# A two-block transformer prologue in fp32: modulation summed beside the projections, differential attention beside the value and half the output projection

## The reference

```python
z, xbc, dt_raw, q, k, v = split_cols(h @ w_in, EVEN_SPLITS)      # h = norm(x) * (1 + scale) + shift
y_ssd = ssd_mixer(z, xbc, dt_raw, conv_w, conv_b, dt_bias, A_log, D_skip, ssd_norm)
y_diff = diff_attention(q, k, v, lam, diff_norm, rel_bias, layer_idx)
return jnp.concatenate([y_ssd, y_diff], axis=-1) @ w_out

# diff_attention, causal, 8 heads, two maps m of 64 features each
logits = einsum("bqhmd,bkhmd->bhmqk", q_blk, k32) + bias[None, :, None]
p = softmax(where(dist >= 0, logits, -inf))
attn = p[:, :, 0] - lam_full * p[:, :, 1]
out = rms_norm(einsum("bhqk,bkhe->bqhe", attn, v32), subln_w) * (1.0 - lam_init)
```

## Time and profile before

| what | us |
|---|---|
| device time, median of 3 runs | 4331.51 (4325.75 to 4333.39) |
| the profiled execution | 4334.11 |
| its span, first to last instruction | 4332.2 |
| TensorE busy in the span | 3752.1 (87%) |
| VectorE, ScalarE, GpSimd busy | 1823.6, 1319.7, 457.8 |
| granted TensorE clock, mean | 0.887 |
| moved by DMA | 313.45 MB |

### The profile page before, as it was taken

One profiled execution on the slowest core, in us unless ns is written; L12 is line 12 of the kernel. 1 busy time (PEld: TensorE's weight loads), 2 busy tenths in 40 slices (PEclk: granted clock), 3 DMA queues, 4 the chain that ended last, 5 costly groups with the idle time before them and its releaser, 6 DMA issues. The chain is left out here.

```text
span 4332.2 us, 48721 instructions
## 1 busy us (share of the span) xinstructions
PE 3752.1 (87%) x19465; PEld 2867.3 (66%) x19465; DVE 1823.6 (42%) x2952; ACT 1319.7 (30%) x2062; POOL 457.8 (11%) x401
## 2 busy tenths in 40 slices
PE   4599866999999479999599887999979988889998
PEld 4487644788868346888466643778856764467886
DVE  5635435333332343332345243445345424344434
ACT  0133224323232233232332233334233114333333
POOL 0000100011000310110113000031001310003100
PEclk6599986999999859999799696999989978689998
DMA  7622110222221002221210001232212100023221
GB/s 281 240 74 69 34 50 32 104 78 88 87 92 54 20 29 88 98 91 65 87 54 31 21 1 54 67 108 88 98 49 73 31 22 1 31 76 102 88 97 39
DMA packets 226412, 313.45 MB, mean 72 GB/s; under 512 B 11925, under 2 KB 151070, under 8 KB 225438
## 3 DMA queue, kind: packets, MB, share of 16 engines
q1 hardware_dynamic: 226206, 310.54, 21.3%
HBM read 306.83 MB, written 3.68 MB: 72 GB/s over the span
## 5 line engine op out<-in xcount | busy, mean ns | idle before, releaser
L373 PE MATMUL out<-h_lo,w_hi 128*128 128x512 f32 x2672 | 1072.1, 401 | 58.0 <-DVE w_lo L364 31.3
L364 DVE TENSOR_TENSOR w_lo<-ring,w_hi 128x1024 fp32r<-128x1024 f32 (+2 forms) x473 | 581.2, 1234 | 1130.8 <-ACT w_hi L359 1125.6
L374 PE MATMUL out<-h_hi,w_hi 128*128 128x512 f32 x2672 | 1051.0, 393 | 0.0
L375 PE MATMUL out<-h_hi,w_lo 128*128 128x512 f32 x2672 | 1050.2, 393 | 0.0
L359 ACT ACTIVATE w_hi<-ring 128x1024 fp32r<-128x1024 f32 (+2 forms) x473 | 483.9, 1028 | 1231.5 <-PE out L375 1131.1
L373 PEld LDWEIGHTS out<-h_lo,w_hi 128*128 128x128 f32 x2672 | 508.3, 190 | 184.2 <-issue 70.4
L374 PEld LDWEIGHTS out<-h_hi,w_hi 128*128 128x128 f32 x2672 | 508.7, 190 | 114.9 <-issue 11.0
L375 PEld LDWEIGHTS out<-h_hi,w_lo 128*128 128x128 f32 x2672 | 507.9, 190 | 107.4
L373 PE MATMUL item_banks<-h_lo,w_hi 128*128 128x512 f32 (+1 forms) x632 | 283.3, 448 | 4.9 <-DVE w_lo L364 4.9
L375 PE MATMUL item_banks<-h_hi,w_lo 128*128 128x512 f32 (+1 forms) x632 | 251.9, 399 | 0.0
L374 PE MATMUL item_banks<-h_hi,w_hi 128*128 128x512 f32 (+1 forms) x632 | 251.7, 398 | 0.0
(11 more groups left out here) (484 smaller groups left out, 4915.4 us busy)
## 6 DMA issues: line engine op xcount, KB each, us to landing
ring<-in_mlp_w SPq DMA_DIRECT2D x30, 2048.0 KB, 8.4
ring<-in_mod_w SPq DMA_DIRECT2D x24, 2048.0 KB, 8.0
ring<-in_w_up SPq DMA_DIRECT2D x44, 1024.0 KB, 6.5
ring<-in_e_w_in SPq DMA_DIRECT2D x44, 512.0 KB, 4.0
ring<-in_w_in SPq DMA_DIRECT2D x22, 1024.0 KB, 5.2
ring<-in_w_down SPq DMA_DIRECT2D x10, 2048.0 KB, 7.8
ring<-in_o_w_in SPq DMA_DIRECT2D x7, 2048.0 KB, 7.9
ring<-in_w_ple_gate SPq DMA_DIRECT2D x4, 2048.0 KB, 8.4
```

What stands on the lines that cost most here:

```text
L364: return nc.vector.tensor_tensor(lo.bitcast(F32R), x, hi, ALU.subtract)
L373: nc.tensor.matmul(out, wh, xl, start=start, stop=False, **kw)
L374: nc.tensor.matmul(out, wh, xh, start=False, stop=False, **kw)
L375: return nc.tensor.matmul(out, wl, xh, start=False, stop=stop, **kw)
```

## The change

- `load_inputs`, `modulation`, `relative_bias` and `lambda_stage` go, and with them `project`. A region `opening` loads, turns x, sums its squares and takes the root, computes the bias list and lambda, and sums only the shift and scale of the first sublayer: 8 chunks of 128 x 2048 (1 MB), each multiplied and added by one VectorE instruction.
- The other ten (sublayer, part) pairs are blocks of 8 chunks of 128 x 1024 (512 KB), through a ring of two slots. Six blocks are summed on VectorE in the scan region, planned one chunk each 4.1 us; four on GpSimd in the new attention region, one each 4.5 us. Each block ends in an item of kind "sums" of 8 one-column matmuls in the item stream.
- `shift_lane` applies gain and shift in the scan region, without the statistics.
- The bias is read for each head as a window of a DRAM array `bias_rows` that holds the list 128 times, the causal mask in it (NEG past the diagonal). The odd mixer reads its band from there.
- `even_attention` is one region of the value projection (8 row items), the scan half of the output projection (8 feature items, written over the scan's output), the split of that half, four blocks of modulation, and `diff_lane`: the 32 units, with two PSUM banks of logits, one for each map of one unit.
- `even_tail` projects 2 blocks instead of 4 and adds the stored half to each output tile before squaring.

```diff
+def opening(k, a, tiles, scratch, neg_lam, out_gain):
+        @lane.sync
+            sp.dma_start(k.const[:, :], a["const"]).then_inc(const_in, 16)
+            for g, first, n, src in rows:
+                sp.dma_start(vec_rows[first:first + n, g, :], src).then_inc(rows_in, 16)
+            for c in range(TC):
+                sp.dma_start(x_rows[:, c, :], a["x"][0, c * P:(c + 1) * P, :]).then_inc(x_in, 16)
...
+            for c in range(DT):
+                if c >= 4:
+                    sp.wait_ge(summed, c - 3)
+                sp.dma_start(ring[:, c % 4, :], w[0, :, c, 0:2 * D]).then_inc(w_in[c % 4], 16)
+            sp.wait_ge(values_out, 1)
+            sp.wait_ge(masked, 1)
+            sp.dma_start(k.bias_rows.ap(), values.unsqueeze(1).to_broadcast([HEADS, P, S + P])).then_inc(values_kept, 16)
+        @lane.vector
...
+                nc.vector.tensor_copy(k.xT[:, f, :], banks[:, f % 6, :]).then_inc(x_out, 1)
...
+            dve.wait_ge(c_done, 1)
+            for c in range(DT):
+                dve.wait_ge(w_in[c % 4], 16 * (c // 4 + 1))
...
+                    step = nc.vector.scalar_tensor_tensor(acc, ring[:, c % 4, :], k.c_act[:, c:c + 1], acc, ALU.mult, ALU.add)

+def modulation_lane(k, r, lane, name, a, blocks, ring, acc, begin, pace, taken, on_pool=False):
+    @lane.sync
+        for n in range(CHUNKS):
+            yield begin + pace * (n - U)
+            if n >= U:
+                sp.wait_ge(summed, n - U + 1)
+            sp.dma_start(ring[:, n % U, :], w[s, :, c, part * D:(part + 1) * D]).then_inc(landed[n % U], 16)
+    if on_pool:
...
+                nc.gpsimd.tensor_scalar(slot, slot, gain_of(c), None, ALU.mult).then_inc(scaled, 1)
+                pool.wait_ge(scaled, b * (DT - 1) + c)
+                pool.wait_ge(summed, n)
+                nc.gpsimd.tensor_tensor(total, total, slot, ALU.add).then_inc(summed, 1)
+    else:
+                yield begin + pace * n
+                sums(dve, n)                              # waits for landed
...
+                nc.vector.scalar_tensor_tensor(total, slot, gain_of(c), total, ALU.mult, ALU.add).then_inc(summed, 1)

 def items_lane(...)                                     # TensorE
+            for wait in item.ready:
+                pe.wait_ge(*wait)
+            if item.kind == "sums":
+                for q in range(DT):
+                    last = nc.tensor.matmul(banks[:, m % 2, q:q + 1], item.moving[:, q * P:(q + 1) * P], k.at["ones"][:, 0:1], start=True, stop=True)

+def diff_lane(k, r, lane, qT, kT, v_rows, v_ready, neg_lam, out_gain, mixT, banks, BEGIN, UNIT):
+    def unit(n):
+        h, qb = divmod(n, TC)
+        return h, qb, (qb + 1) * P, BEGIN + UNIT * n
+    # TensorE
+            steps += [(at, "score", n), (at + 6.2, "turn", n), (at + 7.8, "mix", n)]
+            if what == "score":
+                for m in range(2):
+                    if n >= 1:
+                        pe.wait_ge(shifted, 2 * n - 1 + m)
+    # VectorE
+            steps += [(at + 0.8, "shift", n), (at + 4.2, "mix", n)]
+    # ScalarE
+            steps += [(at + 1.6, "exp", n), (at + 7.0, "copy", n)]

+def even_scan(k, a, xbc, qT, kT, scratch):
+        BEGIN, PACE = 7.5, 4.1
+        blocks = [(0, 2), (1, 0), (1, 1), (1, 2), (2, 0), (2, 1)]
+        sums = modulation_lane(k, r, r.lane(0.0, 1.0), "mod", a, blocks, mod_ring, mod_acc, 14.0, PACE, taken)
+            while sums and at >= 14.0 + PACE * DT * (len(blocks) - len(sums) + 1) + 3.0:
+                placed.append(sums.pop(0))
+            item.begin, item.length = at, 8.6 if item.kind == "feat" else 5.6

+def even_attention(k, a, xbc, qT, kT, neg_lam, out_gain):
+        blocks = [(2, 2), (3, 0), (3, 1), (3, 2)]
+        PACE = 4.5
+        sums = modulation_lane(k, r, r.lane(0.0, 1.0), "mod", a, blocks, mod_ring, mod_acc, 6.0, PACE, taken, on_pool=True)
+            item.begin, item.length = at, 11.5 if item.kind == "feat" else 6.0 if at < 18.0 else 7.8
+        diff_lane(k, r, r.lane(0.0, 1.0), qT, kT, v_rows, v_ready, neg_lam, out_gain, qT, banks, 11.5, 4.75)

 def residual_lane(...)                                  # VectorE
+            if partial is None:
+                nc.vector.tensor_copy(ch.y0, out[:, 0, :]).then_inc(y0_kept, 1)
+            else:
+                nc.vector.tensor_tensor(partial[:, f, :], out[:, f, :], partial[:, f, :], ALU.add).then_inc(y0_kept, 1)

 def even_tail(...)
-        outs, _ = down_blocks(a["e_w_out"][0], (4, 4, 4, 4))
+        outs, _ = down_blocks(a["e_w_out"][0][D:2 * D], (4, 4))
```

More of the change, by code:

```diff
@@ L268, in _ @@
[L268 to L274, removed]
-        def _(dve):
+            pe.wait_ge(tab_in, 32)
+            nc.tensor.matmul(banks[0:HEADS, 6, :], tab[:, 0:HEADS], tab[:, HEADS:], start=True, stop=True).then_inc(values_done, 1)
+            pe.wait_ge(x_out, 3)
@@ new lines, in _ @@
+            for f in range(DT):
+                pe.wait_ge(squared, f + 1)
+                last = nc.tensor.matmul(banks[:, 2, :], k.at["ones"], sq[:, f, :], start=(f == 0), stop=(f == DT - 1))
+            last.then_inc(stat_done, 1)
+            pe.wait_ge(summed, DT)
+            pe.wait_ge(x_out, 4)
+            for q in range(2 * DT):
+                last = nc.tensor.matmul(banks[:, 3, q:q + 1], acc[:, q * P:(q + 1) * P], k.at["ones"][:, 0:1], start=True, stop=True)
+            last.then_inc(cols_done, 1)
@@ L283, in _ @@
-        @block.scalar
+                nc.vector.tensor_copy(k.xT[:, f, :], banks[:, f % 6, :]).then_inc(x_out, 1)
+            dve.wait_ge(values_done, 1)
+            nc.vector.tensor_copy(values[:, 0:S], banks[0:HEADS, 6, :]).then_inc(values_out, 1)
+            dve.wait_ge(lam_in, 16)
+            for i in range(2):
+                if i:
+                    dve.wait_ge(dot_done, i)
+                nc.vector.tensor_tensor_reduce(lam_tmp, lam[:, 2 * i, :], lam[:, 2 * i + 1, :], 1.0, 0.0, ALU.mult, ALU.add,
+                                               dots[:, i:i + 1]).then_inc(dot_done, 1)
@@ L592, in run @@
-def run(n_tiles, w_tile, evac, rows=False, after=None, parts=1):
-    return n_tiles, w_tile, evac, rows, after, parts
-def pairs(eng, n_tiles, body):
-    looped = (n_tiles - 1) // 2
-    if looped < 3:
-        looped = 1
-    for t in range(min(2, n_tiles)):
-        body(0, t, t == n_tiles - 1)
-    if looped >= 3:
-        with eng.Fori(1, looped) as i:
-            for u in range(2):
-                body(i, u, False)
-    for t in range(2 * looped, n_tiles):
-        body(t // 2, t % 2, t == n_tiles - 1)
@@ L685, with __init__, left, items_lane @@
 class Item:
[L688 removed]
+    def __init__(self, kind, load, at, width, out, chunks=(), scale=None, tile=0, func=None, moving=None, ready=(), each=()):
         self.kind, self.load, self.at, self.width, self.out = kind, load, at, width, out
[L690 removed]
+        self.chunks, self.scale, self.tile, self.func, self.moving, self.ready, self.each = chunks, scale, tile, func, moving, ready, each
         self.begin, self.length = 0.0, 0.0
[L694 removed]
+def left(freed, m):
+    return freed[m % 2], m // 2 + 1
+def items_lane(k, r, lane, w, ranges, items, h_ready, ring, w_hi, w_lo, banks, tap=None, bias=None, quick=False):
     nc = k.nc
[L697 removed]
+    views = [x.rearrange("(k p) n -> p k n", p=P) for x in (w if isinstance(w, list) else [w] * len(ranges))]
     HELD = w_hi.shape[2] // P
@@ L740, in leave @@
         item = items[m]
-        if item.func is not None:
+        if item.kind == "sums":
+            step = nc.vector.tensor_tensor(item.out, view(m), item.scale, ALU.add)
+        elif item.func is not None:
             step = nc.scalar.activation(item.out, view(m), item.func)
```

939 lines of the change are left out of this document (414 added, 525 removed).

## The result

| | before | after |
|---|---|---|
| median of the runs, us | 4331.57 (4325.75 to 4333.39) | 4215.3 (4209.97 to 4223.19) |
| ratio | 1 | 0.9732, 95% interval 0.9721 to 0.9744 |
| profiled execution, us | 4334.11 | 4209.97, span 4208.2 |

The account below looks back on a forecast made before the run. TensorE was taken to bound convolutions and output projection, while modulation loads, norm and attention left engines idle or waiting. Terms -148 + 22 - 58 + 3 = -181 took 4334.1 to 4153, less 2.6: 4150 us, range 4100 to 4212.

Parts of the forecast that it names:

- Part 1: Opening: scan region begins at 51 instead of 190, low weights 9.2 earlier; -148 us, between -157 and -134.
- Part 2: Scan region: modulation chunks on VectorE and one-column matmuls on TensorE add 22 us, between 8 and 45.
- 2.5 are spare: Scan region: a bank is needed 5.6 after its item, tap and three taps take about 0.7 + 3 x 0.8.
- Part 3: Attention, values and half the output: new region 206 us replaces 264.2; -58, between -84 and -29.
- Part 4: Tail: squares after an addition, and a gating step that may block with GpSimd; +3 us, 0 to 6.
- (b): Rival, chance 0.19: VectorE bounds scan and attention regions, convolution items lengthen, GpSimd's chunk takes 6.2; region 235, time 4199.
- (a): Rival, chance 0.20: GpSimd hardly disturbs the attention, VectorE's passes fall between its waits for loads; region 180, time 4124.
- (c): Rival, chance 0.02: chunk landings decide, each waited for in VectorE's fixed order; at a landing of 12.5, time 4374.
- (d): Rival, chance 0.04: TensorE reaches the sums before they are ready, modulation stays exposed; 10 in each of ten sums, 4250.

Follow-up runs that it names:

- side bank: The changed kernel with the scan region's modulation sums that fall among row and convolution items in their own PSUM bank: 4211.9 us, ratio 0.9715.

## Why the prediction was wrong

Against the profiled execution I had 4334.1 - 181 = 4153; it took 4210.0. (Between the medians it is 65: the profiled execution is 5 below the changed kernel's median, and 4153 less 2.6 was given as 4150.) The 57 are, by the parts:

- **Part 1, the opening: the failed step.** "The list written to DRAM 128 times (2.6 MB) is issued near 33 and hides behind this chain; if it reads too slowly from its 8 partitions it comes out as the end instead, up to 14 later." It came out as the end, 38.6 us after the chain. The chain itself was right to 3.3 (47.2 for 50.5), region to first projection too (10.65 for 10.3). So 34.8 of the miss are this one transfer: -104 where -139 stood. I had named the mechanism and its condition, but gave it 14 with no row behind the figure (the upper end of the part, -148 + 14 = -134) and left it out of the sum. The nearest landings were reads into 128 partitions (8.0 for 2 MB); none of them bounds a transfer from 8, and an unbounded cost should have widened the range. With this step mended alone, by the write from 128 partitions, the time is 4179.9, inside the range; the 30 that are left against 4150 are mainly part 3.
- **Part 2, the scan region: the total near, by other terms, so in part by luck.** 25.4 against 22. The convolution items keep their 5.6, as forecast; up to the scan 13.2 were lost and in it 12.2. But each of the two sums between two convolutions costs 5.0, not 1.8: I counted its matmuls and not the bank. With two banks in turn, a short item gives the item behind it only 1.8 us until it needs the bank of the convolution just ended, whose taps still read it for 3.1. My own "2.5 are spare" held for items of 5.6 only. Behind the wait nine matmuls ran at a granted clock of 0.54, which the side bank took away too.
- **Part 3, the attention region: 230.0 for 206,** 24 of the miss (up to 32 by the other executions with this code), and its two terms were wrong in opposite directions. The unit without GpSimd was put at 4.2; it is 5.6 (206.6 us without any sums). I had built it from VectorE's chain, "with one unit of logits in flight", while half of the missing time ((5.6 - 4.2) x 31 = 43) was TensorE's order: later transposes and value products take 22 us off and leave a unit of 4.9. GpSimd's disturbance was put at 26.5 x 1.85 = 49 us; with the sums' matmuls and loads it is 23.4 in the profiled executions (230.0 - 206.6) and 37 by the ratios, although GpSimd holds the way longer than I had it. Its one-input pass takes 3.24 where I chose 1.2 by the nearer kind (a copy), so a chunk takes 6.3 instead of 5.0, and GpSimd works for 202 us, 84% of them busy, instead of 160 at 72%. Of the 40 us by which VectorE's instructions grow, a part falls into the waits of that ring. That L1351 is blocked too, which I had assumed with no row for it, is now seen: L1209 of 128 columns, which takes 0.29 us with the sums on VectorE, started beside an addition of GpSimd's, took 2.12 and ended just behind it. The Trainium skill (SBUF — State Buffer, "Who interferes with whom") says this of VectorE's two-port modes, and the trace agrees.

```profile
642.18 2.37 POOL L422 TENSOR_TENSOR mod_acc<-mod_acc,mod_ring 128x1024 f32<-128x1024 f32 x1
...
642.51 2.12 DVE L1209 TENSOR_SCALAR diff_probs<-diff_probs,diff_weight 128x128 f32<-128x128 f32 x1
644.67 0.35 DVE L1211 SCALAR_TENSOR_TENSOR diff_probs<-diff_probs,diff_weight 128x128 f32<-128x128 f32 x1
```

- **Part 4, the tail: -2 for +3.** From the first output matmul to the first one of the MLP it is 1.0 longer (73.54 for 72.59 without two blocks), less than the 3; another 3.1 are less behind it. Neither can be told from the spread: from the tail's first matmul to the end, code that no run changed, the kernels after took 3521 to 3537 us.

Sum: 34.8 + 0.4 + 3.4 + 24 - 5 = 57.6. Of the rivals, (b) was nearest in number (4199, region 235) and in GpSimd's work (6.2 a chunk and 198 us, measured 6.3 and 202), though its conditions in the convolution did not come: the items kept 5.6. (a) fell: the mixes grew from 30.1 to 65.3 us. (c) and (d) did not come either: chunks landed in 3.7 to 4.5 and VectorE waited 8.4 us for them in all, and TensorE waited for no chunk's sum ahead of its one-column matmuls.

## What to carry to other kernels

Look for the partitions that a transfer reads, not only for its bytes: 2.6 MB written from 8 partitions took over 50 us, from 128 of them 12.9; and a transfer that slow was not hidden by issuing it later in a queue that the other loads share. Where three engines hand a unit around, first look at which in-order queue has the next unit's first step behind this unit's last; here it was the value product ahead of the next score but one. Moving it behind gave 14 us with the disturbing engine still at work and 33 without it; taking the sums off that engine gave 20. The two hide in each other, so each has to be tried with and without the other. And before an order is judged, look whether the new planned times change it at all. A short item in a two-bank rotation costs the time until the previous item's bank is free, and what the clock loses in that wait: 5.0 us for 1.8 of matmuls.

## What the runs showed of the hardware that was not expected

- A transfer of 2.6 MB from 8 partitions moves 50 GB/s at a DMA share of 0.47, and a 512 KB load issued behind it landed after 46 us instead of 5 to 6. The same bytes from 128 partitions moved at 413 GB/s and a share of 1.03: twice the engines, and each piece in 102 ns instead of 382.
- GpSimd multiplies 1024 columns by a per-partition scalar in 2.84 us at best, by a repeated second input in 1.89, and adds two inputs in 2.34: the form with fewer inputs is the slowest. The kernel with the faster form was slower.
- VectorE multiplied a whole 128x1024 chunk by a scalar in 0.75 us, against 1.28 for the multiply-add (sums on VectorE), so the first chunk of a block is nearly half price.
